# Value projections of head groups two and three: tokens taken four apart by the matmul's stationary operand

## Chip, core and metric

One NeuronCore of a Trainium2 chip runs the whole kernel. The metric is the device time of one execution in microseconds (us). The kernel before takes 1042.13 us, the median of three runs (1041.59 to 1042.42).

## What is computed

One layer of a decoder, for a prompt of 512 tokens and for 32 sample tokens (8 sequences of 4). The part that matters here:

```python
h = rmsnorm(x); z = h @ w_in            # columns: u | va | q | k | v | gates
# branch B: 3 head groups (window, dilation) = (128,1), (512,4), (2048,16), 8 heads of 64 each
q, k = rotary(rmsnorm(q)), rotary(rmsnorm(k))
# prompt, group with dilation d: tokens of the same residue mod d attend to each other
o = softmax(mask(q k^T / 8)) @ v
# outputs besides y: the k and v rows of every group (kv128_prompt, kv512_prompt, kv2048_prompt)
```

For the groups with dilation 4 and 16 the kernel works on the four residues of the token number modulo 4. A residue has 128 of the 512 tokens, so a head is four 128 x 128 score blocks. For dilation 16 a mask inside the block leaves the pairs that are a multiple of four apart within it.

## The kernel before

**Order of the work.** The projection is split in panels of 256 columns of `w_in` (half a head group of q, k or v), and a panel in units. For q, k, v and va ("natural" panels, tokens on partitions) a panel has three units: sub 0 and sub 1 hold two tiles of 128 prompt tokens each, sub 2 the 32 sample tokens. TensorE runs the units strictly in order, numbered as slots: q, k, v of group one (slots 0 to 17), of group two (18 to 35), of group three (36 to 53), then va, u, the gates and so on. Group two is called g = 1 in the code, group three g = 2. The value units of g = 1 are slots 30, 31 (i = 0) and 33, 34 (i = 1), those of g = 2 are slots 48, 49 and 51, 52. Between the matmuls of a unit TensorE runs small steps of the attention (transposes, scores, products with V) that belong to the slot before; they are laid out by hand in the code at fixed slots.

**One natural unit** (`natural_unit`, lines 1324 to 1354). Activations and weights are split in two fp32r parts (`h_hi`, `h_lo`, `w_hi`, `w_lo`). For each of the two token tiles and each of the 8 blocks k of the contraction there are three matmuls (lines 1341, 1342, 1343), with 128 tokens of `h_hi` or `h_lo` as the stationary operand (128 columns, loaded by a LDWEIGHTS of its own before each matmul) and 256 columns of weights as the moving operand. That is 2 x 8 x 3 = 48 loads and 48 matmuls. `h_hi[:, k, tile]` is 128 adjacent fp32 values in each partition. Lines 1349 and 1350 are the sample unit: a stationary operand of 64 columns (`hs`), 16 matmuls.

**Where V comes from.** ScalarE evacuates each value unit from PSUM into `V[g % 2]` (line 873), a tile of `[128, 4 tiles, 8 heads, 65]` fp32, and stores the two token tiles to the output `kvp{g}` (line 883, two DMAs issued by ScalarE's queue per unit for g > 0, 16 in all). At that point V holds tokens 128a to 128a+127 in its tile a. The attention of groups two and three needs the tokens a, a+4, a+8, ... in tile a. So SyncE's queue (SP) waits until the stores of a half group have landed, at the slots of

```python
V_BACK = {35: (1, 0), 39: (1, 1), 53: (2, 0), 57: (2, 1)}
```

and reads the half group back from `kvp{g}` with the rows rearranged, over the same V tile, four DMAs each time (line 701, 16 in all). The semaphores `v_residues` tell TensorE that they have landed; `values(j)` waits for them at the first head of each half group (lines 1541, 1542) and then multiplies `PT` (stationary) by V (line 1546 for groups two and three, line 1554 for group one).

**Other queues around it.** The same SP queue loads the weight panels (`w_raw`, line 636), the cache chunks of the sample attention (`kv`, line 648) and query rows (line 657), in program order. ScalarE rounds `w_raw` to `w_hi` (line 760), VectorE makes `w_lo` (line 1728) and does the sample attention (lines 1947, 1948 on keys; 1988, 1994 on values) and, in `mask_weights` and `sum_weights`, reduces `sc` over its middle axis (lines 1962, 1976: elements 8 fp32 apart) and subtracts the maximum (line 1966: adjacent elements). Line 1016 (ScalarE) and line 2146 (VectorE) write or read `x2_hi`/`x2_lo` with elements four fp32 apart; lines 1072 and 2209 are their counterparts on adjacent elements. Lines 1459 and 1467 are transposes, four products of 128 columns each; line 1588 is a warming product at the start, line 1428 the first transposes of x.

Of the kernel before, what the change touches and what calls it, by code (L numbers as in the profile page):

```python
# [58 lines left out]
UNIT = {}  # L59
# [179 lines left out]

SLOTS = U_FF  # L240
COPY_AT = [s for s in range(0, 96, 3) if s not in (48, 51, 54, 57)] + [97, 99, 100, 102]
V_BACK = {35: (1, 0), 39: (1, 1), 53: (2, 0), 57: (2, 1)}


X_STEPS = {10: (2,), 13: (3,), 14: (4,)}
# [79 lines left out]
def build(nc, t):  # L325

    ctx = ExitStack()
    with ctx:
# [135 lines left out]
        fin_stored = [sem("fin_stored0"), sem("fin_stored1"), sem("heads_stored")]  # L464
        gelu_arg, gelu_tanh = sem("gelu_arg"), sem("gelu_tanh")
        v_stored = [[sem(f"v_stored{g}_{i}") for i in range(2)] for g in range(NG)]
        vn_stored, v_residues = [sem(f"vn_stored{g}") for g in range(NG)], [sem(f"v_residues{i}") for i in range(2)]

        t_ready, t_out, s_ready, max_ready = sem("t_ready"), sem("t_out"), sem("s_ready"), sem("max_ready")
        mask_written = sem("mask_written")  # L470
# [151 lines left out]
        def _(sp):  # L622
# [49 lines left out]
            for s in range(SLOTS):  # L672
                p, kind, g, i, sub = UNITS[s]
                if sub == 0 and p + 1 < len(PANELS) and s != 54:
                    load_panel(p + 1)
                if s == 52:
                    load_panel(p + 2)
                if s == 0:
                    for i, name in ((1, "g_ffn"), (2, "g_ple")):
                        sp.dma_start(gcol[:, i], t[name].rearrange("(k p) -> p k", p=128),  # L680
                                     allow_slow_non_contiguous=True).then_inc(const_in, 16)

                if s == 4:
                    sp.wait_ge(h_lo_done, KD + 1)
                if 4 <= s < 4 + RING:
                    sp.wait_ge(unit_ready, s - 1)
                    load_chunk(s - 4)
                if s == 10:
                    load_queries(0)
                for g in range(1, NG):  # L690
                    if s == max(KEYS_END[g - 1] + 3, UNIT["q", (g, 1, 2)] + 6):
                        load_queries(g)
                for n in range(RING, NCH):
                    if s == CH_SLOT[n - RING] + 3 and CHUNKS[n][1] < 2:
                        load_chunk(n)
                if s in V_BACK:
                    g, i = V_BACK[s]
                    sp.wait_ge(v_stored[g][i], V_STORES[g])
                    src = t[f"kvp{g}"][1].rearrange("(n a) (h d) -> n a h d", a=4, d=HD)
                    for a in range(4):  # L700
                        sp.dma_start(V[g % 2][:, a, 4 * i:4 * i + 4, 0:HD], src[:, a, 4 * i:4 * i + 4]).then_inc(v_residues[i], 16)
                if 45 <= s < 49:
                    a = s - 45
                    sp.wait_ge(o_out, 16)
                    for b in range(4):
                        sp.dma_start(O0[32 * b:32 * b + 32, a], O_blk[a:128:4, b]).then_inc(o_moved, 16)
                if s == 51:
                    sp.wait_ge(pv_ready, 24)
                    sp.wait_ge(o_moved, 256)
                    wait_values(sp, 1)  # L710
                    sp.dma_start(ws_nat[:], t["w_s"].rearrange("g t s -> t g s")).then_inc(ws_in, 16)
                    sp.dma_start(fold[:], t["c_fold"]).then_inc(const2_in, 16)
                    sp.dma_start(same_b, t["c_same"]).then_inc(const2_in, 16)
                if s == 59:
                    sp.dma_start(gv_b[:], t["g_v"].partition_broadcast(128)).then_inc(const2_in, 16)
                    sp.dma_start(bs_b[:], t["b_s"].partition_broadcast(128)).then_inc(const2_in, 16)
                if s == 86:
                    sp.wait_ge(values_used, kind_count(NCH - 1))
                    sp.dma_start(xn[:], t["x_prompt"].rearrange("(b p) d -> p b d", p=128)).then_inc(x2_in, 16)
                    sp.dma_start(xs[:], t["x_sample"]).then_inc(x2_in, 16)  # L720
                if s == 89:
                    sp.wait_ge(t_ready, TINDEX[("sb",)] + 1)
                    sp.dma_start(pn[:], t["p_prompt"].rearrange("(b p) d -> p b d", p=128)).then_inc(p_in, 16)
                    sp.dma_start(pns[:], t["p_sample"]).then_inc(p_in, 16)
# [21 lines left out]
        def _(act):  # L746
# [83 lines left out]
            def evacuate(u):  # L830
# [22 lines left out]
                elif kind in ("k", "q", "va"):  # L853
                    r = stage_slot(u)
                    if sub == 2:
                        nc.scalar.copy(sq[0:NS, r, 256:512], gm[NS:2 * NS, u % 3, 0:256]).then_inc(lo_rows, 1)
                    else:
                        if kind == "va":
                            nc.scalar.activation(sq[:, r, 0:n], src, ACT.Square, scale=GELU_A ** 0.5).then_inc(sq_ready, 1)
                        nc.scalar.copy(z[:, r, 0:n], src).then_inc(unit_out, 1)  # L860
                        if kind != "va":
                            act.wait_ge(unit_out, u + 1)
                            square_heads(u, slice(0, 128), slice(0, 128), z[:, r], 8, r)
                elif kind == "u":
                    r = stage_slot(u)
                    nc.scalar.activation(two(sq[:, r]), src, ACT.Square, scale=GELU_A ** 0.5).then_inc(sq_ready, 1)
                    nc.scalar.copy(two(z[:, r]), src).then_inc(unit_out, 1)
                elif kind == "v":
                    if sub < 2:
                        if g == 2 and i == 0 and sub == 0:  # L870
                            wait_values(act, 0)
                            act.wait_ge(pv_ready, 16)
                        nc.scalar.copy(V[g % 2][:, 2 * sub:2 * sub + 2, 4 * i:4 * i + 4, 0:HD],
                                       src.rearrange("p (t h d) -> p t h d", t=2, h=4)).then_inc(unit_out, 1)
                    else:
                        nc.scalar.copy(Sn[0:NS], gm[NS:2 * NS, u % 3, 0:256]).then_inc(lo_rows, 1)
                    if sub < 2:
                        act.wait_ge(unit_out, u + 1)
                    cols = slice(256 * i, 256 * i + 256)
                    if sub < 2 and g > 0:  # L880
                        for x in range(2 * sub, 2 * sub + 2):
                            dst = t[f"kvp{g}"][1, 128 * x:128 * x + 128, cols].rearrange("p (h d) -> p h d", h=4)
                            act.dma_start(dst, V[g % 2][:, x, 4 * i:4 * i + 4, 0:HD]).then_inc(v_stored[g][i], 16)
                    elif sub == 1:
                        dst = t["kvp0"][1, :, cols].rearrange("i (h d) -> i h d", h=4)
                        act.dma_start(dst, V[0][:, 3, 4 * i:4 * i + 4, 0:HD]).then_inc(v_stored[g][i], 16)
                elif kind in ("ga", "gb"):
                    if kind == "ga":
                        m = 2 * i + sub
                        if m == 0:  # L890
                            act.wait_ge(exp_done, 32)
                            act.wait_ge(pv_ready, 32)
                            act.wait_ge(va_sq, 5)
                        if m == 4:
                            act.wait_ge(z_used, zc(UNIT["oa", 3]))
                        out = tha[:, m % 4]
                    else:
                        m = 2 * i + sub
                        if m == 0:
                            act.wait_ge(b_ready, 1)  # L900
                            act.wait_ge(t_ready, TINDEX[("bt", 3)] + 1)
                        out = thb[:, m]
                    nc.scalar.activation(two(out), src, ACT.Tanh, scale=0.5).then_inc(unit_out, 1)
                elif kind == "pj":
                    if sub == 0:
                        act.wait_ge(h_lo_done, HP)
                    nc.scalar.copy(two(proj[:, sub]), src).then_inc(unit_out, 1)
                else:
                    r = stage_slot(u)
                    nc.scalar.copy(two(z[:, r]), src).then_inc(unit_out, 1)  # L910
# [379 lines left out]
        def _(pe):  # L1290
# [33 lines left out]
            def natural_unit(u):  # L1324
# [4 lines left out]
                for x in range(2 if sub < 2 else 1):  # L1329
                    for k in range(KD):  # L1330
# [2 lines left out]
                        if sub == 0 and x == 0:  # L1333
                            panel_split(p, n, k)
                        if sub < 2:
                            tile = slice(128 * (2 * sub + x), 128 * (2 * sub + x) + 128)
                            lh, ll = h_hi[:, k, tile], h_lo[:, k, tile]
                            out = gm[:, u % 3, n * x:n * x + n]
                        wh, wl = w_hi[:, r, k * n:k * n + n], w_lo[:, r, k * n:k * n + n]
# [194 lines left out]
            def values(j):  # L1534
# [4 lines left out]
                if j == 0:  # L1539
                    pe.wait_ge(zeroed, 1)  # L1540
                if g and hd % 4 == 0:
                    pe.wait_ge(v_residues[hd // 4], 64 * g)
                W = HD + 1
                if g:
                    for a in range(4):
# [1041 lines left out]
```

## Time and profile before

| | |
|---|---|
| median of three runs | 1042.13 us (1041.59 to 1042.42) |
| the profiled execution's own time | 1042.98 us |
| its span, first to last instruction | 1040.9 us |
| mean granted TensorE clock | 0.996 of full |
| TensorE matmul busy | 1023.7 us, 98% |
| weight loads busy | 1009.4 us, 97% |
| VectorE, ScalarE, GpSimd busy | 766.8, 519.7, 242.2 us |
| DMA | 195.89 MB, 131,794 packets |
| V stores by ScalarE's queue (groups two and three) | 16 DMAs of 128 KB |
| V read back by SP's queue | 16 DMAs of 128 KB |

The profile is one execution, recorded by the hardware. PE is TensorE's matmul, PEld its weight load, DVE VectorE, ACT ScalarE, POOL GpSimd, SP SyncE; a q behind the name is the engine's sequencer issuing DMAs. Matmuls are pipelined, so the duration of one is its latency, and the pace of a stream is read from the distance of two starts or from many of them divided by their number. "Idle before" is the time an engine stood before an instruction and what released it.

### The profile page before, as it was taken

The page shows a single profiled execution, that of the slowest core. Times are in us where ns is not written, and L with a number is a line of the kernel's source. Part 1 is how long each engine was busy: PE and PEld are TensorE (multiplying, and loading weights), DVE is VectorE, ACT ScalarE, POOL GpSimd, SP SyncE. Part 2 cuts the span into 40 slices and gives each one's busy share as a digit, 9 for nine tenths or more (in the row PEclk, how much of TensorE's full clock was granted, in tenths as well). Part 3 has the DMA queues.
Part 4 walks back from the last instruction along what each step waited for, and adds up shares of the span by engine and source line. Part 5 has one row for each costly group of instructions (what it writes and reads, how often), then busy time and mean ns, then how long its engine had stood idle before and what let it go on. Part 6 is the DMA issues. An engine that isn't in the chain of part 4 may idle for free.

```text
span 1040.9 us, 20870 instructions
## 1 busy us (share of the span) xinstructions
PE 1023.7 (98%) x8310; PEld 1009.4 (97%) x8310; DVE 766.8 (74%) x994; ACT 519.7 (50%) x1253; POOL 242.2 (23%) x384
## 2 busy tenths in 40 slices
PE   9999999999999999999999999999999999999997
PEld 7999999999999999999999989999999999999997
DVE  6579798988999778999674368747856875786553
ACT  6773797659835564352354385414522531453332
POOL 3441233113322003958201211100100100012300
PEclk9999999999999999999999999999999999999999
DMA  6556656686787755776833336555754575573412
GB/s 186 195 175 227 209 174 208 226 246 204 231 242 219 216 197 156 222 211 195 268 122 116 127 122 210 212 183 172 232 206 154 194 248 167 171 252 130 156 59 86
DMA packets 131794, 195.89 MB, mean 188 GB/s; under 512 B 32481, under 2 KB 109633, under 8 KB 129906
## 3 DMA queue, kind: packets, MB, share of 16 engines
q1 hardware_dynamic: 107776, 125.51, 38.2%
q0 software_dynamic: 10560, 63.28, 18.0%
q10 hardware_dynamic: 13362, 5.77, 2.0%
q8 instruction: 66, 1.08, 0.4%
q14 instruction: 30, 0.25, 0.1%
HBM read 185.55 MB, written 62.00 MB: 238 GB/s over the span
## 4 chain that ended last, share of the span: by engine, by line
PE 78%; DVE 10%; ACT 4%; issue 3%; POOL 2%; DMA 2%; DVEq 0%; ACTq 0%; POOLq 0%
PE gm L1367 24%; PE gm L1623 7%; PE gm L1341 7%; PE gm L1342 6%; PE gm L1343 6%; PE psSO L1623 4%; PE psT L1623 3%; PE psSO L1671 2%; PE psSO L1367 2%; PE psT L1367 2%; PE psT L1671 2%; POOL kv L2410 2%; DVE w_lo L1728 2%; PE gm L1349 1%; PE gm L1350 1%
## 5 line engine op out<-in xcount | busy, mean ns | idle before, releaser
L1341 PE MATMUL gm<-w_hi,h_hi 128*128 128x256 f32 x640 | 186.5, 291 | 0.4 <-DVE w_lo L1734 0.4
L1342 PE MATMUL gm<-w_hi,h_lo 128*128 128x256 f32 x640 | 180.5, 282 | 0.0
L1343 PE MATMUL gm<-w_lo,h_hi 128*128 128x256 f32 x640 | 179.8, 281 | 0.0
L1367 PE MATMUL gm<-h_hi,w_hi 128*128 128x272 f32 x624 | 133.1, 295 | 0.0
L1367 PE MATMUL gm<-h_hi,w_lo 128*128 128x272 f32 x624 | 130.3, 290 | 0.0
L1367 PE MATMUL gm<-h_lo,w_hi 128*128 128x272 f32 x624 | 129.7, 290 | 0.0
L1341 PEld LDWEIGHTS gm<-w_hi,h_hi 128*128 128x128 f32 x640 | 120.6, 188 | 2.2 <-issue 0.8
L1343 PEld LDWEIGHTS gm<-w_lo,h_hi 128*128 128x128 f32 x640 | 121.1, 189 | 0.0
L1342 PEld LDWEIGHTS gm<-w_hi,h_lo 128*128 128x128 f32 x640 | 120.4, 188 | 0.0
L2399 POOL DMA_DIRECT2D out_kvs<-in_cache_kv_w x64 | 35.0, 547 | 345.0 <-PE gm L1367 121.0
L1728 DVE TENSOR_TENSOR w_lo<-w_raw,w_hi 128x1024 fp32r<-128x1024 f32 x76 | 90.2, 1227 | 22.7 <-ACT w_hi L760 22.5
L1367 PEld LDWEIGHTS gm<-h_hi,w_hi 128*128 128x128 f32 x624 | 98.7, 190 | 0.8
L1367 PEld LDWEIGHTS gm<-h_lo,w_hi 128*128 128x128 f32 x624 | 99.0, 190 | 0.0
L1367 PEld LDWEIGHTS gm<-h_hi,w_lo 128*128 128x128 f32 x624 | 98.6, 191 | 0.0
L770 ACT CAST w_hi<-w_raw 128x1024 fp32r<-128x1024 f32 x49 | 50.1, 1046 | 82.5 <-PE psSO L1367 28.5
L760 ACT CAST w_hi<-w_raw 128x1024 fp32r<-128x1024 f32 x76 | 76.8, 1047 | 25.9 <-DMA w_raw<-in_w_in 15.4
L1367 PE MATMUL gm<-x_hi,w_hi 128*128 128x272 f32 x384 | 80.3, 290 | 0.0
L1367 PE MATMUL gm<-x_hi,w_lo 128*128 128x272 f32 x384 | 79.5, 288 | 0.0
L1367 PE MATMUL gm<-x_lo,w_hi 128*128 128x272 f32 x384 | 79.2, 288 | 0.0
L2410 POOL DMA_DIRECT2D kv<-in_cache_kv_w x128 | 69.5, 702 | 32.7 <-DVE acc L1994 16.8
L1741 DVE TENSOR_TENSOR w_lo<-w_raw,w_hi 128x1024 fp32r<-128x1024 f32 x49 | 59.0, 1221 | 11.9 <-ACT w_hi L770 11.8
L1367 PEld LDWEIGHTS gm<-x_lo,w_hi 128*128 128x128 f32 x384 | 60.3, 189 | 0.0
(385 smaller groups left out, 2650.5 us busy)
## 6 DMA issues: line engine op xcount, KB each, us to landing
out_kvs<-in_cache_kv_w POOLq DMA_DIRECT2D x64, 510.0 KB, 4.6
w_raw<-in_w_in SPq DMA_DIRECT2D x60, 512.0 KB, 6.1
w_raw<-in_w_ff SPq DMA_DIRECT2D x36, 512.0 KB, 5.5
kv<-in_cache_kv_w SPq DMA_DIRECT2D x128, 128.0 KB
kv<-in_cache_kv_w SPq DMA_DIRECT2D x64, 256.0 KB
out_kvs<-in_cache_kv_w POOLq DMA_DIRECT2D x32, 508.0 KB, 5.1
w_more<-in_w_ff SPq DMA_DIRECT2D x26, 512.0 KB, 5.9
kv<-in_cache_kv_w POOLq DMA_DIRECT2D x128, 64.0 KB, 3.3
```

Source lines behind the costliest of these rows:

```text
L760: nc.scalar.copy(w_hi[:, r, hh * 1024:(hh + 1) * 1024], w_raw[:, hh]).then_inc(w_hi_done, 1)
L770: nc.scalar.copy(w_pair(w_hi, PAIRS[p] + n).rearrange("p (k n) -> p k n", k=4), raw(p, hh)).then_inc(w_hi_done, 1)
L1341: nc.tensor.matmul(out, lh, wh, start=k == 0, stop=False)
L1342: nc.tensor.matmul(out, ll, wh, start=False, stop=False)
L1343: last = nc.tensor.matmul(out, lh, wl, start=False, stop=k == KD - 1)
L1367: last = nc.tensor.matmul(pair[:, half, 0:HALF], w, x[:, k0 + k, half * HALF:(half + 1) * HALF], start=first, stop=end)
L1623: last = nc.tensor.matmul(bank[:, 0:HALF], w[wx][:, k], x[xx][:, k], start=start and k == 0 and wx == xx, stop=k == 3 and wx == 1, skip_gr ...
L1671: last = nc.tensor.matmul(banks(u + sub)[:, half, 0:HALF], w, x[:, k, half * HALF:(half + 1) * HALF], start=first, stop=end, skip_group_ch ...
L1728: vec.tensor_tensor(w_lo[:, r, cols], w_raw[:, hh], w_hi[:, r, cols].bitcast(F32), ALU.subtract).then_inc(w_lo_done, 1)
L1741: vec.tensor_tensor(w_pair(w_lo, x).rearrange("p (k n) -> p k n", k=4), raw(p, hh), w_pair(w_hi, x).rearrange("p (k n) -> p k n", k=4).bit ...
L2399: pool.dma_start(dst, src).then_inc(cache_copied, 16)
L2410: pool.dma_start(dst, src).then_inc(late_landed[n % RING], 16)
```

## The change

The stationary operand of the value units of groups two and three takes tokens a, a+4, ..., a+508 for tile a, instead of 128 adjacent ones. V then already has the order that the attention needs; the stores go to every fourth row of the output, the read-back is gone with its semaphores, and `values` waits for the evacuation of the half group's second unit. The number of matmuls, of loads and of stores is the same.

```diff
-V_BACK = {35: (1, 0), 39: (1, 1), 53: (2, 0), 57: (2, 1)}
...
-                if s in V_BACK:
-                    g, i = V_BACK[s]
-                    sp.wait_ge(v_stored[g][i], V_STORES[g])
-                    src = t[f"kvp{g}"][1].rearrange("(n a) (h d) -> n a h d", a=4, d=HD)
-                    for a in range(4):
-                        sp.dma_start(V[g % 2][:, a, 4 * i:4 * i + 4, 0:HD], src[:, a, 4 * i:4 * i + 4]).then_inc(v_residues[i], 16)
...
                         for x in range(2 * sub, 2 * sub + 2):
-                            dst = t[f"kvp{g}"][1, 128 * x:128 * x + 128, cols].rearrange("p (h d) -> p h d", h=4)
+                            dst = t[f"kvp{g}"][1, x:SEQ:4, cols].rearrange("p (h d) -> p h d", h=4)
                             act.dma_start(dst, V[g % 2][:, x, 4 * i:4 * i + 4, 0:HD]).then_inc(v_stored[g][i], 16)
...
                         if sub < 2:
-                            tile = slice(128 * (2 * sub + x), 128 * (2 * sub + x) + 128)
+                            a = 2 * sub + x
+                            tile = slice(a, SEQ, 4) if kind == "v" and g else slice(128 * a, 128 * a + 128)
                             lh, ll = h_hi[:, k, tile], h_lo[:, k, tile]
...
                 if g and hd % 4 == 0:
-                    pe.wait_ge(v_residues[hd // 4], 64 * g)
+                    pe.wait_ge(unit_out, UNIT["v", (g, hd // 4, 1)] + 1)
```

The semaphores `v_residues` are no longer allocated.

## Rows read from the trace of the kernel before

**Rows 1.** The page: busy time of the engines over the span.

```profile
span 1040.9 us, 20870 instructions
PE 1023.7 (98%) x8310; PEld 1009.4 (97%) x8310; DVE 766.8 (74%) x994; ACT 519.7 (50%) x1253; POOL 242.2 (23%) x384
```

**Rows 2.** Tile V: duration min/median/max in ns, first and last start; then its waiters.

```profile
L883 ACTq DMA_DIRECT2D out_kvp<-V x16: 374/454/937, 184.6 to 312.1; - x16
L701 SPq DMA_DIRECT2D V<-out_kvp x16: 440/1666/3133, 210.5 to 341.1; - x16
...
  PE gm L1588: 1.6, 1
```

**Rows 3.** Windows: us, then busy (instructions) of each engine, clock, DMA share, GB/s.

```profile
290.00:300.00 10.00, 10.00 (x87) 10.00 (x86) 9.73 (x13) 5.86 (x14) 1.42 (x2) 1.00 0.74 224
300.00:310.00 10.00, 10.00 (x86) 10.00 (x85) 9.80 (x10) 2.69 (x3) 0.67 (x1) 1.00 0.97 261
```

**Rows 4.** Groups of weight loads by form: count, busy us, mean ns of one.

```profile
L1341 PEld LDWEIGHTS gm<-w_hi,h_hi 128*128 128x128 f32 x640 | 120.6, 188 | 2.2 <-issue 0.8
L1349 PEld LDWEIGHTS gm<-w_hi,hs 128*64 128x64 f32 x160 | 21.5, 134 | 0.5
```

**Rows 5.** ScalarE's timeline: start us, duration us, the evacuations after slots 51, 52.

```profile
305.39 0.59 ACT L873 COPY V<-gm 128x512 f32<-128x512 f32 x1 [5.39 <-PE gm L1343]
...
311.04 0.59 ACT L873 COPY V<-gm 128x512 f32<-128x512 f32 x1 [1.52 <-PE gm L1343]
```

**Rows 6.** The chain that ended last: start us, duration us, 128-column loads with short matmuls.

```profile
242.88 0.84 PE psSO L1546 x8
```

**Rows 7.** VectorE groups by form: elements far apart (L1962, L2146) and adjacent (L1966, L2209).

```profile
L1962 DVE TENSOR_REDUCE sm<-sc 128x8 f32<-128x264 f32 x1 | 0.7, 686 | 0.0
L1962 DVE TENSOR_REDUCE sm<-sc 128x8 f32<-128x136 f32 x1 | 0.4, 421 | 0.0
...
L1966 DVE TENSOR_TENSOR sc<-sc,sm 128x264 f32<-128x264 f32 x2 | 0.9, 432 | 0.1
L1966 DVE TENSOR_TENSOR sc<-sc,sm 128x136 f32<-128x136 f32 x1 | 0.3, 299 | 0.0
...
L2146 DVE TENSOR_TENSOR x_lo<-sq,x_hi 128x512 fp32r<-128x512 f32 x4 | 4.4, 1119 | 0.4 <-ACT sq L1018 0.3
L2209 DVE TENSOR_TENSOR pT_lo<-sqf,pT_hi 128x512 fp32r<-128x512 f32 x2 | 1.4, 684 | 0.0
```

**Rows 8.** ScalarE groups by form: the same contrast in SBUF writes.

```profile
L1016 ACT CAST x_hi<-psT 128x512 fp32r<-128x512 f32 x4 | 4.4, 1112 | 0.0
...
L1072 ACT CAST h_hi<-psT 128x512 fp32r<-128x512 f32 x4 | 2.2, 588 | 4.4 <-PE psT L1428 4.4
```

**Rows 9.** SP's timeline: start us, duration us, the read-backs.

```profile
210.55 4.47 SPq L701 DMA_DIRECT2D V<-out_kvp  x4
235.29 7.23 SPq L701 DMA_DIRECT2D V<-out_kvp  x4
315.84 7.81 SPq L701 DMA_DIRECT2D V<-out_kvp  x4
335.07 7.71 SPq L701 DMA_DIRECT2D V<-out_kvp  x4
```

**Rows 10.** Waits from 180 to 375 us: us in total, times, longest.

```profile
DVE fin L1881 <- POOL st L2453: 4.3, 4, 1.3
DVE z L1892 <- ACT sq L856: 4.0, 2, 2.3
DVE va L1921 <- ACT sq L923: 3.2, 1, 3.2
...
ACT w_hi L760 <- DMA w_raw<-in_w_in: 1.9, 3, 1.1
```

**Rows 11.** TensorE's timeline: its two longest pauses after the value units.

```profile
351.09 0.63 PE L1467 MATMUL psT<-ident,prob 128*128 128x128 f32 x4 [1.56 <-ACT prob L1143]
...
369.09 1.16 PE L1529 MATMUL psSO<-kT,qT 64*128 64x128 f32 x8 [1.70 <-ACT psSO L1150]
```

**Rows 12.** Windows of 5 us around them.

```profile
370.00:375.00 5.00, 5.00 (x29) 4.88 (x28) 4.60 (x6) 2.29 (x7) 0.00 (x0) 0.66 0.56 199
375.00:380.00 5.00, 5.00 (x43) 5.00 (x42) 4.53 (x5) 3.88 (x8) 0.00 (x0) 1.00 0.52 200
```

**Rows 13.** TensorE's timeline at the start of the kernel.

```profile
7.31 3.35 PE L1588 MATMUL gm<-ones 128*128 128x128 f32 x14
...
12.75 1.04 PE L1428 MATMUL psSO<-ident,xn 128*128 128x128 f32 x8
```

More of the change, by code:

```diff
@@ L466, in build @@
         v_stored = [[sem(f"v_stored{g}_{i}") for i in range(2)] for g in range(NG)]
-        vn_stored, v_residues = [sem(f"vn_stored{g}") for g in range(NG)], [sem(f"v_residues{i}") for i in range(2)]
+        vn_stored = [sem(f"vn_stored{g}") for g in range(NG)]
         t_ready, t_out, s_ready, max_ready = sem("t_ready"), sem("t_out"), sem("s_ready"), sem("max_ready")
```

## The prediction

> **What bounds the kernel now.** I read the page first: matmuls are busy 1023.7 of 1040.9 us and weight loads 1009.4 [rows 1]. TensorE is the path, and a change is worth what it does to TensorE's stream. Next the tile view of V, for the read-back that the change removes: 16 DMAs, issued from 210.5 to 341.1 us. Among those who waited for V the only TensorE line is L1588, 1.6 us at the very start, behind a memset [rows 2]. So nobody on the path waits for the read-back. The windows around the last value units show both TensorE columns full, with VectorE at 97 to 98% beside it [rows 3].
>
> Then the question is what one step of a value unit consists of. A step is a load of 128 stationary columns and a matmul of 256. The two evacuations after slots 51 and 52 are 305.39 and 311.04 us apart: 5.65 us for 48 steps, 117.7 ns a step [rows 5]. How much of that is the load? Loads of 128 columns take 188 ns and loads of 64 take 134, so a column costs 54 / 64 = 0.84 ns, and 128 of them 108 ns of work; the rest is latency that overlaps [rows 4]. Directly: eight products with 128-column loads and only 65 moving columns take 0.84 us, 105 ns each, and there only the load can be the limit [rows 6]. So a load fills 105 of the 117.7 ns. It is hidden under the matmul with 12.7 ns to spare and no more.
>
> **The change, part by part.**
>
> *The read-back goes.* 16 issues, four groups of 4.47, 7.23, 7.81 and 7.71 us on SP's queue, 27.2 us together [rows 9]. On the path: nothing [rows 2]. What stood behind it in SP's queue are weight panels, cache chunks and queries. From 180 to 375 us VectorE's long waits are for GpSimd and ScalarE, none for a chunk, and ScalarE waited 1.9 us in all for weights, three times, while TensorE was full [rows 10, 3]. Bound: 0 to 1.9 us of gain; I take 0. If that cover were gone, a late panel would cost its own lateness.
>
> *The stores* have the same number, the same 1 KB rows, and only another row distance. They are issued by ScalarE's queue at the same place, median 454 ns [rows 2], and nothing on the path waits for them before a DMA at slot 51. 0 us.
>
> *The new wait* is for the evacuation of slot 31, 34, 49 or 52, and the first product that needs it comes several slots (of some 6 us) later. Behind it on TensorE stands everything, but the condition is long true. 0 us. The wait for 64 or 128 DMA counts goes; it ended nothing either.
>
> *The strided load.* 8 units of 48 loads, 384 in all, each with elements 16 bytes apart. The trace has no weight load or moving operand like that, so the price is bounded from other engines. VectorE's reduction over elements 32 bytes apart: 686 ns for 264 and 421 for 136, 2.07 ns an element; the subtraction over the same tile, adjacent: 432 and 299, 1.04 ns. Exactly twice. With elements 16 bytes apart, 512 take 1119 ns against 684 adjacent, 0.85 ns more each [rows 7]. ScalarE writing 512 elements 16 bytes apart: 1112 ns against 588, 1.02 ns more each [rows 8].
> - Lower end: the load isn't slowed. 0 us.
> - By the factor of two: 2 x 105 = 210 ns a load. The matmul hides below it, so a step takes 210 instead of 117.7: 92.3 ns x 384 = 35.4 us.
> - By ScalarE's excess: 105 + 1.02 x 128 = 236 ns: 118 x 384 = 45.4 us.
> - Upper end, VectorE's absolute 2.07 ns: 265 ns a load: 147 x 384 = 56.6 us.
>
> I take 35.4: VectorE's rate halves exactly, and a load, like it, takes its elements one by one at a steady rate (0.84 ns a column), so the same factor on TensorE's own rate is nearer than another engine's nanoseconds. The Trainium skill (Advanced Engine Details and Errata, SBUF Cachelines) states that SBUF has lines of 16 bytes, that at least two hits on a line are needed to absorb the access latency, and that a new line at each access has a penalty. Rows 7 and 8 agree, and it speaks against this change. It names no price.
>
> *What is given back.* Each head group has four such units, so TensorE is slower by 4 x 48 x 92.3 ns = 17.7 us in slots 30 to 34, and by as much in slots 48 to 52. Nothing covers that, but VectorE, which is at 97 to 98% there [rows 3] and behind afterwards, catches up meanwhile. What it was late with is seen at 351.09 and 369.09 us, pauses of 1.56 and 1.70 us behind the attention scores [rows 11]; after the second the clock was at 0.66 for 5 us, 29 matmuls instead of 43, 14 x 0.125 = 1.7 us [rows 12]. So 0 to 5.0 us come back; I take 3, since VectorE's load from slot 54 on stays as it is. The later stretch, after 400 us, is set by a chain of its own.
>
> *Sum.* 35.4 - 3 = +32 us. On the profiled execution 1042.98 + 32 = 1075.4 (its span 1040.9 + 32 = 1073.3, 2.1 us of time lying around the span). It lies 0.85 us above the median of the three runs, so against the median the forecast is 1042.1 + 32, rounded 1074 us.
>
> **The rivals.**
>
> *The strided load is free.* TensorE reads SBUF by a path of its own. Its moving operand takes 256 fp32 in about 118 ns, so its reads are at least twice as fast as what a load asks for, and a load may have room for a new line at each element. If so the steps stay at 117.7 ns and nothing else is on the path: 1042.1, say 1041 to 1043, not slower. It decides if a load stays below 117.7 ns, that is if the stride costs less than 12.7 ns, 0.1 ns an element. For it: no row shows TensorE slowed by a pattern. Against it: both engines with such rows pay in full. The Trainium skill (SBUF — State Buffer, in the note on cachelines) says that one may stride for free by 4 fp32, which is the distance here; by that reading the time would be this rival's, but ScalarE's and VectorE's rows at just 4 fp32 contradict it [rows 7, 8].
>
> *A part of the price.* A load of about 157 ns, half as much again, as an overlap with its own latency of some 80 ns would give: 39 x 384 = 15 us, 1057.
>
> *The clock falls.* In a strided unit the array streams 107 of 210 ns. If that counts as idle, loads and matmuls go at the lower of the two speeds, 1.2 GHz. At the start 14 products took 3.35 us, 239 ns each, more than twice the 105 [rows 13, 6]; a strided load would then take some 470 ns: 352 x 384 = 135 us, 1177. Against it: out of just this stretch of one 128-column product in 239 ns the pace rose, to (1.04 - 0.28) / 7 = 109 ns at 12.75 us [rows 13].
>
> *Freed queues make it faster.* SP's 27.2 us and 2 MB of reads are gone, chunks and weights land earlier, and the 1.56 and 1.70 us pauses with their clock loss shrink. With free loads: down to 1042.1 - 1.9 - 3 = 1037. Against it: VectorE at 97 to 98% is late by its own work, not by chunks [rows 3, 10].
>
> **How the numbers follow.** A measurement here can tell about 0.2%, 2.1 us, from no change. Full price of the stride (35 to 57 us, less 0 to 5): 0.62. A part of the price: 0.06. Clock fall: 0.03. Free load, time unchanged: 0.25. Faster: 0.04. Slower is 0.62 + 0.06 + 0.03 = 0.71, same 0.25, faster 0.04. The likeliest case alone runs from 1042.1 + 35.4 - 5 = 1072 to 1042.1 + 56.6 = 1099. Since a quarter lies on no change, the range must take that in: from 1041 to 1092, which leaves out the faster case, the clock fall and the dearest twentieth of the likeliest.
>
> **What would show it.** Right: in the changed profile, loads of lines 1341 to 1343 grow a second duration, some 100 ns above 188, in eight units only; evacuations after slots 51 and 52 stand 48 x 0.21 = 10.1 us apart instead of 5.65; the page's PEld stays near full while VectorE's share between 285 and 330 us falls; the pauses of rows 11 shrink. The read-back's line is gone from the DMA view, and no new wait of TensorE for ScalarE's evacuation appears. Wrong: the same 5.65 us between those evacuations, with the time unchanged; then the load path doesn't share the other engines' limit. If the evacuations are 5.65 apart and the time still differs by more than 2 us, the queues did it, and the waits for `kv` and `w_raw` must have moved.

## The result: slower by 42 us, the steps of eight value units at half their pace

| | before | changed |
|---|---|---|
| median of the runs | 1042.28 us (4 runs, 1041.59 to 1046.12) | 1085.26 us (4 runs, 1082.04 to 1085.71) |
| profiled execution, own time | 1042.98 us | 1085.71 us |
| its span | 1040.9 us | 1083.7 us |
| value unit, step (load and matmul) | 117.7 ns | 234.4 ns |

The ratio is 1.0407, 95% interval 1.0389 to 1.0426, so +42.4 us (40.5 to 44.4).

The page of the changed kernel, its span and its busy times, against [rows 1]:

```profile
span 1083.7 us, 20854 instructions
PE 1067.6 (99%) x8310; PEld 1053.3 (97%) x8310; DVE 765.8 (71%) x994; ACT 520.0 (48%) x1253; POOL 240.1 (22%) x384
...
DMA packets 123346, 193.79 MB, mean 179 GB/s; under 512 B 24033, under 2 KB 101185, under 8 KB 121458
```

Both TensorE columns grew by 44 us with the same number of instructions; the other engines did the same work. 8448 DMA packets are gone.

Its groups of weight loads by form (line, out<-in, shape, count, busy us, mean ns), the former lines 1341 to 1343:

```profile
L1337 PEld LDWEIGHTS gm<-w_lo,h_hi 128*128 128x128 f32 x640 | 139.2, 218 | 0.0
L1336 PEld LDWEIGHTS gm<-w_hi,h_lo 128*128 128x128 f32 x640 | 139.0, 217 | 0.0
L1335 PEld LDWEIGHTS gm<-w_hi,h_hi 128*128 128x128 f32 x640 | 138.4, 216 | 2.7 <-issue 1.3
```

A mean of 217 instead of 188 [rows 4] hides that two kinds are mixed here: of 640 loads on each line 128 belong to the changed units. The timeline of the weight loads inside slot 52 (start us, duration us) shows one of them:

```profile
349.79 0.33 PEld L1335 LDWEIGHTS gm<-w_hi,h_hi 128*128 128x128 f32 x1
350.03 0.34 PEld L1336 LDWEIGHTS gm<-w_hi,h_lo 128*128 128x128 f32 x1
```

0.33 us in place of 0.19 [rows 4], one every 0.24 us. ScalarE's timeline gives the same over a whole unit, the evacuations after slots 51 and 52:

```profile
343.83 0.59 ACT L866 COPY V<-gm 128x512 f32<-128x512 f32 x1 [11.00 <-PE gm L1337]
...
355.08 0.59 ACT L866 COPY V<-gm 128x512 f32<-128x512 f32 x1 [7.60 <-PE gm L1337]
```

11.25 us where [rows 5] had 5.65: 234.4 ns a step. 384 steps at 116.7 ns more are 44.8 us, against 42.8 measured between the spans. The windows over these units (us, busy of PE, PEld, DVE, ACT, POOL, then the clock) answer to [rows 3]:

```profile
330.00:340.00 10.00, 10.00 (x52) 10.00 (x52) 5.21 (x5) 0.95 (x2) 2.04 (x2) 1.00 0.27 74
340.00:350.00 10.00, 10.00 (x44) 10.00 (x43) 3.44 (x3) 2.59 (x3) 0.00 (x0) 1.00 0.22 52
```

TensorE still reads as full, with 44 to 52 matmuls in 10 us instead of 86: the busy share of a pipelined stream says nothing about its pace, the count does. VectorE has gone from 98% to 34 to 52%, as the engine that is now waiting. The clock stayed at 1.00.

### The profile page after: what moved, and what is told of

Read it like the earlier page. It is cut to its first block, busy times and chain, and to the rows that moved or that the text cites. A ratio compares the mean times of both kernels' runs of the same rounds, so it can differ in the third digit from the quotient of the medians.

```text
span 1083.7 us, 20854 instructions
## 1 busy us (share of the span) xinstructions
PE 1067.6 (99%) x8310; PEld 1053.3 (97%) x8310; DVE 765.8 (71%) x994; ACT 520.0 (48%) x1253; POOL 240.1 (22%) x384
## 4 chain that ended last, share of the span: by engine, by line
PE 79%; DVE 10%; ACT 3%; issue 3%; DMA 3%; POOL 2%; SPq 0%; DVEq 0%; ACTq 0%; POOLq 0%
PE gm L1361 23%; PE gm L1335 8%; PE gm L1336 8%; PE gm L1337 8%; PE gm L1617 7%; PE psSO L1617 3%; PE psT L1617 3%; PE psSO L1665 2%; PE psT L1361 2%; PE psSO L1361 2%; PE psT L1665 2%; POOL kv L2404 2%; DVE w_lo L1722 2%; PE gm L1343 1%; PE gm L1344 1%
## 5 line engine op out<-in xcount | busy, mean ns | idle before, releaser
L1335 PE MATMUL gm<-w_hi,h_hi 128*128 128x256 f32 x640 | 201.6, 315 | 0.9 <-DVE w_lo L1728 0.9
L1336 PE MATMUL gm<-w_hi,h_lo 128*128 128x256 f32 x640 | 195.5, 306 | 0.0
L1337 PE MATMUL gm<-w_lo,h_hi 128*128 128x256 f32 x640 | 194.6, 304 | 0.0
L1335 PEld LDWEIGHTS gm<-w_hi,h_hi 128*128 128x128 f32 x640 | 138.4, 216 | 2.7 <-issue 1.3
L1337 PEld LDWEIGHTS gm<-w_lo,h_hi 128*128 128x128 f32 x640 | 139.2, 218 | 0.0
L1336 PEld LDWEIGHTS gm<-w_hi,h_lo 128*128 128x128 f32 x640 | 139.0, 217 | 0.0
```

Source lines behind the costliest of these rows:

```text
L1335: nc.tensor.matmul(out, lh, wh, start=k == 0, stop=False)
L1336: nc.tensor.matmul(out, ll, wh, start=False, stop=False)
L1337: last = nc.tensor.matmul(out, lh, wl, start=False, stop=k == KD - 1)
```

## The experiments

All values are medians, and each ratio is to the kernel before as measured beside that version (medians 1042.53, 1042.76 and 1042.96 us). Single runs of the kernel before lay between 1038.6 and 1047.4, so differences of 1 us are not told apart. A step's time is read from the evacuations after slots 51 and 52 in each profile. The value rows of these kernels are of other tokens or columns than the reference's, or stand in another order; the expectation of each says which.

**Loads alone.** Only the tile of the stationary operand is changed in the kernel before; read-back and old stores stay.

```diff
-                            tile = slice(128 * (2 * sub + x), 128 * (2 * sub + x) + 128)
+                            a = 2 * sub + x
+                            tile = slice(a, SEQ, 4) if kind == "v" and g else slice(128 * a, 128 * a + 128)
```

> The kernel before, with only the stationary operand of the eight value units strided; the read-back, its waits and the old stores stay, so the value rows land in another order than the reference's. Theory (the strided load is the whole loss): 384 steps of 234 ns instead of 117.7, so 1084 to 1086 us like the changed kernel, and 11.25 us between the evacuations of slots 51 and 52. Rival (the missing read-back gives something back in the changed kernel): this one is more than 2 us above the changed kernel, 1087 to 1090. Second rival (the stores to every fourth row cost something there): this one is faster than the changed kernel, below 1083.

Measured 1084.4 us, ratio 1.0397 (1.0381 to 1.0413), and again 11.25 us between the evacuations in ScalarE's timeline:

```profile
344.44 0.59 ACT L873 COPY V<-gm 128x512 f32<-128x512 f32 x1 [11.00 <-PE gm L1344]
355.69 0.59 ACT L873 COPY V<-gm 128x512 f32<-128x512 f32 x1 [7.60 <-PE gm L1344]
```

This one line of the change is the whole loss. It is 0.9 us from the changed kernel, with overlapping intervals: neither rival is seen.

**No read-back.** The changed kernel with adjacent tokens.

```diff
-                            tile = slice(a, SEQ, 4) if kind == "v" and g else slice(128 * a, 128 * a + 128)
+                            tile = slice(128 * a, 128 * a + 128)
```

> The changed kernel with adjacent tokens in the stationary operand: read-back gone, stores to every fourth row, new wait, but V in the natural token order, so the attention of groups two and three multiplies rows of another order. Theory: the read-back was hidden, so 1042 us, within 2 us of the kernel before; TensorE's waits as before. Rival (freed queues and 16 fewer transfers help): 1037 to 1040, with the pauses of 1.56 and 1.70 us at 351 and 369 us smaller. Rival (new stores or wait cost): above 1044.

Measured 1040.23 us, ratio 0.9979 (0.9964 to 0.9994). At the edge between theory (within 2 us of the kernel before) and first rival (1037 to 1040): by the interval, 0.6 to 3.8 us less. The same edit on top of the strided loads went the other way, +0.9 us (1084.4 to 1085.26), so a gain of 2 us from dropping the read-back isn't shown. TensorE's timeline of this kernel shows how little of it is on the path:

```profile
350.33 0.63 PE L1461 MATMUL psT<-ident,prob 128*128 128x128 f32 x4 [1.30 <-ACT prob L1136]
...
368.25 1.16 PE L1523 MATMUL psSO<-kT,qT 64*128 64x128 f32 x8 [1.72 <-ACT psSO L1143]
```

The pauses of [rows 11] are 1.30 and 1.72 us, 0.24 us less together. Where the rest of the 2 us lies wasn't found; it may be scatter.

**Two apart.** `tile = slice(256 * sub + x, 256 * sub + 256, 2)` in the changed kernel.

> The changed kernel with the stationary tokens two apart (8 bytes) within each 256 tokens, so V has another order than the attention wants. Theory (SBUF delivers one 16-byte line per 1.83 ns to the load, and two elements share a line): 64 lines, 117 ns a load, just hidden, 117.7 to 125 ns a step, 1042 to 1045 us. Rival (any elements that are not adjacent are read one line access each): 234 ns a step, 1085 us. Rival (price in proportion to the distance): about 156 to 176 ns a step, 1057 to 1065 us.

Measured 1040.65 us, ratio 0.9981 (0.9969 to 0.9992), the same as with adjacent tokens. ScalarE's timeline:

```profile
305.83 0.59 ACT L866 COPY V<-gm 128x512 f32<-128x512 f32 x1 [5.43 <-PE gm L1337]
311.50 0.59 ACT L866 COPY V<-gm 128x512 f32<-128x512 f32 x1 [2.03 <-PE gm L1337]
```

5.67 us, 118.1 ns a step, as the theory had it. The weight loads in its timeline take 0.20 us, against 0.19 for adjacent ones:

```profile
305.81 0.20 PEld L1335 LDWEIGHTS gm<-w_hi,h_hi 128*128 128x128 f32 x1
```

Eight bytes apart, a load still fits under a matmul of 256 columns. The rival by which all elements that aren't adjacent pay in full (1085 us) has fallen, and so has a price in proportion to the distance as it was put (156 to 176 ns).

**Eight apart.** The stationary operand takes `[400 * k + a : ... : 8]` of h seen as one row.

> The changed kernel with the stationary elements eight apart (32 bytes), taken across the blocks of h, so the value rows are other numbers than the reference's. Theory (one line access per element, whatever the distance beyond a line): 234 ns a step, 1085 us as with four apart. Rival (price grows with the distance, as with alternating banks): more than 300 ns a step, over 1110 us. Rival (something special in a distance of just 16 bytes): below 200 ns a step, under 1072 us.

Measured 1086.53 us, ratio 1.0418 (1.0404 to 1.0432). ScalarE's timeline:

```profile
346.48 0.59 ACT L866 COPY V<-gm 128x512 f32<-128x512 f32 x1 [11.28 <-PE gm L1340]
358.02 0.59 ACT L866 COPY V<-gm 128x512 f32<-128x512 f32 x1 [7.89 <-PE gm L1340]
```

11.54 us, 240.4 ns a step. Twice the distance adds 6 ns to the step, not another doubling: from 16 to 32 bytes the distance hardly matters. The 6 ns stay open.

**Three apart.** `tile = slice(a, a + 384, 3)`.

> The changed kernel with the stationary tokens three apart (12 bytes), tile a being tokens a, a+3, ..., so the value rows are of other tokens than the reference's. With two apart the load was hidden (118 ns a step), with four apart a step took 234 ns, with eight 240. Theory A (a line of 16 bytes is fetched once, 1.83 ns each, and 128 elements three apart lie on 96 lines): 176 ns a step, + 58 ns x 384 = 22 us over the two-apart kernel's 1040.7, 1063 us. Theory B (full rate needs two elements of a line in a row; where an element is alone on its line it costs 1.83 ns, a pair costs 1.83 too): the same 96 lines, 1063. Rival (any distance over 8 bytes pays in full): 234 ns, 1085 us. Rival (up to 12 bytes free): 1041 us.

Measured 1062.44 us, ratio 1.0175 (1.0148 to 1.0202). ScalarE's timeline:

```profile
324.18 0.59 ACT L866 COPY V<-gm 128x512 f32<-128x512 f32 x1 [8.08 <-PE gm L1337]
332.64 0.59 ACT L866 COPY V<-gm 128x512 f32<-128x512 f32 x1 [4.82 <-PE gm L1337]
```

8.46 us, 176.3 ns a step, forecast 176. So the price goes by the lines of 16 bytes that the elements lie on: 128 elements lie on 96 lines here, 176.3 / 96 = 1.84 ns a line, and four apart 234.4 / 128 = 1.83 ns. Two apart it would be 64 lines, an estimate of 117 ns, just under the matmul's 117.7; that load is hidden, so its own time wasn't measured. Theories A and B give the same count for a regular distance and weren't told apart. A price in proportion to the distance up to 16 bytes and level beyond is, at these distances, the same count too.

**One load in three.** `lh` adjacent, `ll` four apart.

> The changed kernel with only the loads of h_lo four apart, those of h_hi adjacent, so the value rows mix tokens: one load in three is slow. Theory (each slow load is paid by itself, 116.7 ns, as nothing runs ahead of it): 128 x 116.7 = 14.9 us over 1040.7, 1055 to 1057 us, triples of 117.7 + 117.7 + 234 = 469 ns. Rival (loads run ahead and the slack of two adjacent ones hides part): at most 2 x 12.7 ns less per triple, 128 x 25 = 3.3 us less, 1052 us. Rival (a change between patterns costs extra): above 1060 us.

Measured 1054.95 us, ratio 1.0099 (1.0071 to 1.0127), next to the theory's 1055 and 3 us above the first rival. The timeline of its weight loads:

```profile
318.02 0.19 PEld L1335 LDWEIGHTS gm<-w_hi,h_hi 128*128 128x128 f32 x1
318.14 0.31 PEld L1336 LDWEIGHTS gm<-w_hi,h_lo 128*128 128x128 f32 x1
318.36 0.21 PEld L1337 LDWEIGHTS gm<-w_lo,h_hi 128*128 128x128 f32 x1
318.50 0.19 PEld L1335 LDWEIGHTS gm<-w_hi,h_hi 128*128 128x128 f32 x1
```

The slot's evacuations are 7.46 us apart (317.92 and 325.38), 466 ns a triple, where 117.7 + 117.7 + 234.4 is 470. The slack of the two fast neighbours hid 4 ns of the slow load and no more.

**Strided moving operand.** Stationary tokens adjacent, 256 weight columns four apart.

```diff
+                        if kind == "v" and g and sub < 2:
+                            c = 1024 * (k // 4) + k % 4
+                            wh, wl = w_hi[:, r, c:c + 1021:4], w_lo[:, r, c:c + 1021:4]
```

> The changed kernel with the stationary tokens adjacent and instead the moving operand (256 weight columns of the eight units) four fp32 apart, so the value columns are others than the reference's. Theory (the 1.83 ns per line of the load is SBUF's, for every reader): 256 x 1.83 = 468 ns a step, + 351 ns x 384 = 135 us, 1175 us. Rival (the moving read has more lines under way): between 1041 (free) and 1100 us. If the moving read is free, the limit is that of the weight load and not of SBUF.

Measured 1083.99 us, ratio 1.038 (1.0351 to 1.041), far from the theory's 1175 and within the rival's 1041 to 1100. The timelines of weight loads and of matmuls:

```profile
350.04 0.21 PEld L1338 LDWEIGHTS gm<-w_hi,h_hi 128*128 128x128 f32 x1
350.27 0.21 PEld L1339 LDWEIGHTS gm<-w_hi,h_lo 128*128 128x128 f32 x1
```

```profile
350.03 0.41 PE L1340 MATMUL gm<-w_lo,h_hi 128*128 128x256 f32 x1
350.27 0.41 PE L1338 MATMUL gm<-w_hi,h_hi 128*128 128x256 f32 x1
```

Now the load is short (0.21) and the matmul long (0.41 instead of 0.28), and a unit takes 11.15 us (343.54 to 354.69), 232.3 ns a step. That is 0.91 ns a line: the moving read gets lines twice as fast as the load does. The theory that one line in 1.83 ns holds for every reader has fallen.

**Both operands strided.** The two edits together.

> The changed kernel with both operands four apart: stationary tokens as changed, and the 256 moving weight columns too, so the value columns are others than the reference's. Alone the strided load made a step of 234 ns and the strided moving operand one of 232 ns. Theory (the two reads don't share a line rate): the longer of the two, about 234 ns, 1084 to 1087 us. Rival (one line rate for both): 128 x 1.83 + 256 x 0.91 = 466 ns a step, + 348 ns x 384 = 134 us, 1175 us. In between: partly shared.

Measured 1085.86 us, ratio 1.0411 (1.0381 to 1.0442). ScalarE's timeline:

```profile
345.86 0.59 ACT L866 COPY V<-gm 128x512 f32<-128x512 f32 x1 [11.18 <-PE gm L1340]
357.18 0.59 ACT L866 COPY V<-gm 128x512 f32<-128x512 f32 x1 [7.68 <-PE gm L1340]
```

11.32 us, 235.8 ns a step: within 1.4 ns the longer of 234.4 and 232.3, not their sum. The two reads don't slow each other here.

**Wide steps, four apart.** Half as many loads, each under a matmul of 512 columns.

```diff
+                        if sub < 2 and kind == "v" and g:
+                            if k % 2 == 0:
+                                out = gm[:, u % 3, 0:512]
+                                wh, wl = w_hi[:, r, k * n:k * n + 512], w_lo[:, r, k * n:k * n + 512]
+                                nc.tensor.matmul(out, lh, wh, start=k == 0, stop=False)
+                                nc.tensor.matmul(out, ll, wh, start=False, stop=False)
+                                last = nc.tensor.matmul(out, lh, wl, start=False, stop=k == KD - 2)
```

> The changed kernel, tokens four apart, but each of the eight units with half as many loads and a moving operand of 512 columns (two neighbouring blocks of weights side by side), so the products are others than the reference's while the number of moving columns is the same: 192 steps. A matmul of 512 columns lasts 213 ns plus the 11 ns that a step of 256 shows beyond its 106.7. Theory (a step is the longer of load, 234 ns, and matmul, 224 ns): 192 x 234 = 44.9 us against 384 x 117.7 = 45.2 before, so 1040 to 1042 us. Rival (load and matmul don't overlap any more at this length, they add up): over 1060 us.

Measured 1043.95 us, ratio 1.0005 (0.9989 to 1.0021). ScalarE's timeline:

```profile
307.07 0.59 ACT L866 COPY V<-gm 128x512 f32<-128x512 f32 x1 [5.45 <-PE gm L1340]
312.65 0.59 ACT L866 COPY V<-gm 128x512 f32<-128x512 f32 x1 [1.45 <-PE gm L1340]
```

5.58 us for 24 steps, 232.5 ns. The loads are slow still, 0.31 us each in the weight-load timeline, but there are half as many, each under a matmul of nearly its own length, and the time is that of the kernel before. It missed the forecast of 1040 to 1042 by 2 us, and stands 3.7 us above the kernel without read-back. Part of that is the stride, by the next experiment; the rest wasn't found.

**Wide steps, adjacent.**

> The wide kernel (half as many loads, moving operand of 512 columns) with adjacent tokens, so that only the load's stride is gone; products are others than the reference's. With four apart a step took 232.5 ns, 1044 us. Theory: there the load (about 234 ns) was barely the bound; with adjacent tokens the matmul is, 213 + 11 = 224 ns a step, 8.5 ns x 192 = 1.6 us less: 1041 to 1043 us. Rival (a step of 512 columns takes some 232 ns whatever the load): the same 1044 us and 232 ns a step.

Measured 1042.77 us, ratio 0.9994 (0.9976 to 1.0012); 5.38 us a unit (304.87 and 310.25), 224.2 ns a step. Without the stride a step is 8.3 ns shorter, as expected (8.5), so the load was the bound in the strided version and the matmul is in this one. The medians differ by 1.2 us, where 192 x 8.3 ns is 1.6.

**Group three alone.** `... if kind == "v" and g == 2 else ...`

> The changed kernel with strided loads in group three only (four units, slots 48 to 52); group two loads adjacent tokens, so its attention multiplies rows of another order. Theory: 192 x 116.7 = 22.4 us over the 1040.2 of the kernel without read-back, less 1 to 2 us that come back at the pauses of 351 and 369 us: 1061 to 1062 us, and the first pause about 0.5 us as in the changed kernel. Rival (the give-back comes from group two's units): the first pause stays at 1.3 to 1.6 us and the time is 1062.6 or more.

Measured 1061.55 us, ratio 1.0183 (1.0156 to 1.021): 21.3 us over the kernel without read-back, where 192 steps at 116.7 ns more are 22.4. Its first pause, for the scores, is 0.49 us where the kernel without read-back has 1.30, as the theory had it:

```profile
372.36 0.63 PE L1461 MATMUL psT<-ident,prob 128*128 128x128 f32 x4 [0.49 <-ACT prob L1136]
```

So slow units in group three are enough to shrink it. The other four units, in group two, make up the remaining 23.7 us to 1085.26, with nothing given back that these medians could show.

The two fastest versions (no read-back, two apart) stand 2 us, 0.2%, below the kernel before, and neither gives the attention its order. A layout of h in which the tokens of a residue lie two apart should load without loss, by the two-apart run; group one and the other units want other orders, and it wasn't tried.

## Why the prediction came out as it did

*TensorE is the path and the read-back is hidden*: right. 0 was taken, with 1.9 us as the bound [rows 10]; the kernel without it has a median 2.3 us lower with adjacent loads and 0.9 us higher with strided ones, around 0 on both sides.

*The load fills 105 of 117.7 ns and has 12.7 to spare* [rows 5, 6]: right, as far as the runs reach: the two-apart load (estimate 117 ns) is hidden at 118.1 ns a step, and 176 and 234 are paid above 117.7.

*The price of the stride* was the term that was mis-sized. The step said: "the same factor on TensorE's own rate is nearer than another engine's nanoseconds", 210 ns, 35.4 us. It measured 234 ns, 44.8 us. ScalarE's excess of 1.02 ns an element [rows 8] had given 236 ns and 45.4 us, which is nearly the result. The factor of two had a weak source: it set a reduction over elements eight apart against a subtraction over adjacent ones, two different operations, while the same operation in both layouts (L2146 and L2209) went from 684 to 1119 ns, a factor of 1.64 [rows 7]. What the runs show is no factor on the load's 105 ns but a price a line: 1.83 ns, three and four apart alike. An adjacent load lies on 32 lines, some 59 ns at that price, so by this count its columns are the limit there and not its lines. ScalarE's absolute time comes near: in the trace of the kernel before its adjacent copies take 588 ns for 512 elements (L1021) and 388 for 256 (L1023), 0.78 an element, so by this estimate 0.78 + 1.02 = 1.80 ns for one on a line of its own, against the load's 1.83. VectorE's 2.07 doesn't. ScalarE's row is a write and the load a read, and no run ties the two, so the agreement may be luck.

*The give-back*: 3 us taken, of 0 to 5. The pauses of the changed kernel, in TensorE's timeline, against [rows 11]:

```profile
394.02 0.63 PE L1461 MATMUL psT<-ident,prob 128*128 128x128 f32 x4 [0.49 <-ACT prob L1136]
...
411.93 1.16 PE L1523 MATMUL psSO<-kT,qT 64*128 64x128 f32 x8 [1.71 <-ACT psSO L1143]
```

The first shrank by 1.07 us, the second not at all, and the clock loss behind it stayed: the window around it,

```profile
410.00:420.00 10.00, 8.29 (x54) 7.95 (x53) 9.21 (x10) 6.01 (x16) 0.00 (x0) 0.83 0.64 227
```

still shows 0.83, as [rows 12] do over 10 us (0.66 and 1.00). With 0.45 us at the later pause for `acc` (2.06 to 1.61) some 1.5 us came back. The spans say 44.8 - 42.8 = 2.0, but 0.6 of that was there before any changed unit ran: the first evacuation into V came at 79.60 us before and at 78.99 in the changed kernel. Against the kernel without read-back the medians differ by 45.0 us, with nothing given back, so a give-back of 0 to 2 us is all that can be said. Nor could the first pause have paid for more. It is 0.46 to 0.49 us in each version slowed by 12 us or more, and TensorE's timeline of the wide strided kernel, only 1.6 us behind the kernel before at slot 52, has it as short:

```profile
351.59 0.63 PE L1468 MATMUL psT<-ident,prob 128*128 128x128 f32 x4 [0.48 <-ACT prob L1136]
```

The prediction took both pauses for VectorE's lateness, which 35 us of extra time would cover. The second pause is 1.7 us in every kernel run here, with the value units slow or fast, so it isn't a backlog from them; what makes it wasn't tried.

*Stores and the new wait*: 0 and 0, and the loads-alone kernel, which has neither, stands within 0.9 us of the changed one. No wait of TensorE for ScalarE's evacuation of V appears in the changed trace.

*The rivals.* Free loads: fell, at a distance of 16 bytes. The Trainium skill's reading of it (SBUF — State Buffer, the note on cachelines), free by 4 fp32, isn't what the runs show: 2 fp32 are free under this matmul, 3 cost half the price, 4 all of it (118.1, 176.3 and 234.4 ns a step). Its other sentence, at least two hits on a line, agrees with all of them. A part of the price (1057): fell; at this distance the price was paid in full. Clock fall: didn't happen, the granted clock is 1.00 in all windows of the strided units, and a step took 234 ns and not some 470. Faster through freed queues: not seen beyond the 2 us above, and covered by the loss.

So the forecast of 1074 had the side and the mechanism, and its +32 was 10 us short of the measured +42: 9 in the load's price (35.4 against 44.8) and about 1 in the give-back (3 against 2). One sum was written loosely: 1075.4 and 1073.3 carry 32.4, not the 32 that stands beside them; nothing rests on it.

## What to carry to other kernels

Before striding a stationary operand, count the 16-byte lines that its elements lie on: 1.83 ns each was the load's price here, and it is free only while lines x 1.83 stays below the matmul that hides it (some 0.42 ns a moving column and 11 more, an estimate from 117.7 ns at 256 columns and 224.2 at 512), so a distance of two fp32 cost nothing, a moving operand of 512 columns hid all but 8 ns, and what sticks out is paid in full, load by load. A hidden read-back of 2 MB was cheaper than 384 loads that were 117 ns too long, since the read-back was off TensorE's path and the loads are on it. Of the other engines' rows ScalarE's excess in nanoseconds came nearest (236 ns); VectorE's gave 214 (its excess of 0.85 ns an element) and 265. One case doesn't make that a rule: such rows bounded the price, and a run with the one line changed gave it.

## What the runs showed of the hardware that was not expected

- The moving operand pays too, but half: 256 elements four apart take 232.3 ns, 0.91 ns a line, against 1.83 for the load.
- The two reads don't slow each other: both strided, a step takes 235.8 ns.
- Eight apart costs 6 ns a step more than four apart (240.4 and 234.4).
- The price sets in gradually, with the lines touched: 118.1 ns a step two apart (hidden), 176.3 three apart, 234.4 four apart.
- Beside a strided load or moving operand the busy share of TensorE stays at 100% in the windows; only the number of instructions in a window and the distance of their starts show the loss.
